# Fused bias, slope and maximum in two attention layers of a six-layer transformer kernel

## What is computed

```
# layer 3: 8 heads, two maps m per head, head width 64, values of width 128
p = masked_softmax(q_m @ k_m.T - slopes * dist, dist >= 0)
a = p[:, :, 0] - lam_full * p[:, :, 1]
o = rms_norm_2(a @ v, sub_gain) * (1.0 - lambda_init)      # per head of 128
return (o * silu(z)) @ w_out

# layer 4: 3 groups (w, d) = (128,1), (512,4), (2048,16), 4 heads, values of width 256
for each group:  s = q_g @ k_g.T - slopes * dist   on keys with dist <= w, dist % d == 0
                 e = exp(s - m);  l = sum(e);  out_g = (e / l) @ v;  lse_g = m + log(l)
o = sum_g softmax(lse)_g * out_g
return (o * silu(z)) @ w_out
```

## Time and profile before

| | us |
|---|---|
| median of 3 runs | 2045.27 (2043.88 to 2045.29) |
| the profiled execution | 2042.26 |
| its span | 2040.5 |
| TensorE busy | 1742.2 (85%), 9822 matmuls |
| VectorE busy | 1156.1 (57%), 1857 instructions |
| ScalarE busy | 970.5 (48%), 1683 instructions |
| GpSimd busy | 101.1 (5%) |

### The profile page before, as it was taken

One profiled execution on the slowest core, in us unless ns is written; L12 is line 12 of the kernel. 1 busy time (PEld: TensorE's weight loads), 2 busy tenths in 40 slices (PEclk: granted clock), 3 DMA queues, 4 the chain that ended last, 5 costly groups with the idle time before them and its releaser, 6 DMA issues.

```text
span 2040.5 us, 24999 instructions
## 1 busy us (share of the span) xinstructions
PE 1742.2 (85%) x9822; PEld 1379.4 (68%) x9822; DVE 1156.1 (57%) x1857; ACT 970.5 (48%) x1683; POOL 101.1 (5%) x135
## 2 busy tenths in 40 slices
PE   5996878994699973898899998988889969989987
PEld 2783447773577763666799997866678637757866
DVE  2217674446588865764566667435753484464454
ACT  5213223625588865464344443535555534544563
POOL 0000100001100002100000002000000000000000
PEclk7998888997899996999899998998999989999998
DMA  7224996011999982202255554432035303514521
GB/s 304 83 101 167 348 339 247 1 44 59 367 423 421 421 325 95 102 1 83 94 188 188 188 185 144 172 117 83 1 113 187 143 1 134 188 60 147 193 83 42
DMA packets 52691, 335.84 MB, mean 165 GB/s; under 512 B 5488, under 2 KB 5488, under 8 KB 18288
## 3 DMA queue, kind: packets, MB, share of 16 engines
q1 hardware_dynamic: 46112, 310.04, 40.6%
q0 software_dynamic: 6480, 24.44, 3.1%
HBM read 305.10 MB, written 29.36 MB: 164 GB/s over the span
## 4 chain that ended last, share of the span: by engine, by line
PE 66%; DVE 13%; ACT 10%; DMA 6%; issue 3%; POOL 1%; SPq 0%; POOLq 0%; DVEq 0%; ACTq 0%
PE bank L1235 17%; PE bank L1237 17%; PE bank L1236 17%; DMA ring_float<-weights_dram 4%; ACT hT_float L730 2%; DVE ring_float32r L2074 2%; ACT arena_float L784 2%; PE bank L1269 1%; PE bank L1432 1%; ACT ring_high L683 1%; PE bank L1558 1%; PE bank L1606 1%; PE bank L1550 1%; DVE stat L2741 1%; PE bank L1395 1%
## 5 line engine op out<-in xcount | busy, mean ns | idle before, releaser
L2074 DVE TENSOR_TENSOR ring_float32r<-ring_float,ring_high 128x1024 fp32r<-128x1024 f32 x298 | 355.3, 1230 | 369.3 <-ACT ring_high L683 369.1
L683 ACT ACTIVATE ring_high<-ring_float 128x1024 fp32r<-128x1024 f32 x298 | 301.4, 1059 | 412.9 <-DMA ring_float<-weights_dram 410.4
L1235 PE MATMUL bank<-ring_high,x_float32r 128*128 128x512 f32 x608 | 243.4, 400 | 5.6 <-DVE mix_float32r L2103 3.0
L1237 PE MATMUL bank<-ring_high,mix_float32r 128*128 128x512 f32 x608 | 241.2, 397 | 0.0
L1236 PE MATMUL bank<-ring_float32r,x_float32r 128*128 128x512 f32 x608 | 241.1, 397 | 0.0
L1235 PE MATMUL bank<-ring_high,arena_float32r 128*128 128x512 f32 (+1 forms) x368 | 139.6, 379 | 17.3 <-DVE arena_float32r L2103 6.6
L1235 PE MATMUL bank<-Z_float32r,ring_high 128*128 128x256 f32 x512 | 146.0, 285 | 8.0 <-issue 4.2
L1236 PE MATMUL bank<-Z_float32r,ring_high 128*128 128x256 f32 x512 | 146.1, 285 | 0.0
L1237 PE MATMUL bank<-Z_float32r,ring_float32r 128*128 128x256 f32 x512 | 145.9, 285 | 0.0
L1235 PEld LDWEIGHTS bank<-ring_high,x_float32r 128*128 128x128 f32 x608 | 116.0, 191 | 34.6 <-ACT hT_float L730 5.7
L1237 PE MATMUL bank<-ring_high,arena_float32r 128*128 128x512 f32 (+1 forms) x368 | 137.9, 375 | 0.0
(11 more groups left out here) (405 smaller groups left out, 3330.2 us busy)
## 6 DMA issues: line engine op xcount, KB each, us to landing
ring_float<-weights_dram SPq DMA_DIRECT2D x234, 1024.0 KB, 4.8
Z_float<-weights_dram SPq DMA_DIRECT2D x33, 1024.0 KB, 8.7
sent<-post_row SPq DMA_DIRECT2D x1, 11776.0 KB, 38.1
Z_float<-sent SPq DMA_DIRECT2D x23, 512.0 KB, 9.1
made<-mix_float POOLq DMA_DIRECT2D x23, 512.0 KB, 7.9
post_row<-norm_post_dram POOLq DMA_DIRECT2D x4, 512.0 KB, 4.4
small<-small_dram SPq DMA_DIRECT2D x1, 1072.0 KB, 9.2
x_float<-x_dram SPq DMA_DIRECT2D x1, 1024.0 KB, 5.3
```

Of the source, the lines that this page charges most:

```text
L683: nc.scalar.activation(ring_high[:, slot, half], ring[:, slot, half], ACT.Copy).then_inc(high_ready, 1)
L1235: nc.tensor.matmul(out, left[0], right[0], start=start, stop=False)
L1237: return nc.tensor.matmul(out, left[1], right[0], start=False, stop=stop)
L2074: ve.tensor_tensor(ring_low[:, slot, half], ring[:, slot, half], ring_high[:, slot, half], ALU.subtract).then_inc(low_ready, 1)
```

## The change

In layers 3 and 4, bias, slope and row maximum become one VectorE instruction, `tensor_tensor_reduce`: `out = (scores + bias) * (-slope)`, and the minimum of `out`, started from a given value, is written to one element per row. For this the queries are scaled by 1/slope when the banks are emptied (for each head, from a constant in layer 3 and from six new columns of the dilated table in layer 4), and the exponentials are taken with scale -1. A new pair of semaphores `e_full`, `e_free` (`E`, on the same banks 4 and 5) replaces `s_full`, `s_free` there; ScalarE waits for two releases instead of `max_ready`. In layer 4 the minimum of the first map starts the second's, and so on, each with a wait for the one before.

In layer 3 the squares and their sums by head move from VectorE to ScalarE (`head_sums`, four activations of 128 columns with accumulator, after steps 9, 13, 17 and at the end). VectorE's `squares` becomes `values`: reciprocal and scaling, a wait, and a one-element memset that tells ScalarE. The gain and `1 - lambda_init` are multiplied into silu(z) once, in the projection, after the low part of chunk 8 (two instructions of 1024 columns). The norm becomes four instructions of 128 columns, (value * root) * gated z, and comes one unit later.

In layer 4 VectorE no longer adds the three maps. TensorE multiplies the three maps by the identity into the same bank, summing them as it turns them (`turn_sum`), and waits for ScalarE's maps directly.

```diff
-DILATED, N_DILATED = fields([("dilated", 3 * LT * S), ("earlier_keys", P), ("later_sum", P), ("whole_sum", P)])
+DILATED, N_DILATED = fields([("dilated", 3 * LT * S), ("earlier_keys", P), ("later_sum", P), ("whole_sum", P),
+                              ("dilated_q", 6)])
...
+        E = Banks(bank[4:6], e_full, e_free)
...
+            def q_features_by(dst, n_ft, scale_of):
+
+                for j in range(n_ft // 2):
+                    drain(*[(dst[:, f * LT * P:(f + 1) * LT * P], lambda b, f=f: b[:, f % 2 * LT * P:(f % 2 + 1) * LT * P], scale_of(f), None)
+                            for f in (2 * j, 2 * j + 1)])
...
-                            q_features(aq, n_ft, LT, QSCALE)
+                            if i == 3:
+                                q_features_by(aq, n_ft, lambda f: QSCALE / alibi(8)[f])
+                            elif i == 4:
+                                act.wait_ge(dilated_loaded, 16)
+                                q_features_by(aq, n_ft, lambda f: dilated_q[:, f:f + 1])
...
+                def head_sums(g):
+
+                    act.wait_ge(head_values, g + 1)
+                    for n in range(4):
+                        at = slice(g % 2 * 512 + n * 2 * HD, g % 2 * 512 + (n + 1) * 2 * HD)
+                        m = nc.scalar.activation(weighed[:, n * 2 * HD:(n + 1) * 2 * HD], mix[:, g // 2, at], ACT.Square,
+                                                 accum_out=head_ss[:, 4 * g + n:4 * g + n + 1])
+                    m.then_inc(sums_ready, 1)
...
-                        seen.next(max_ready)
+                        seen.next(e_free, 2)
...
+                    if u >= 9 and u % 4 == 1:
+                        head_sums((u - 9) // 4)
+                head_sums(3)
...
+                def turn_sum(u, b):
+                    nk = P * (u // 4 + 1)
+                    for j in range(u // 4 + 1):
+                        for g in range(3):
+                            i = nc.tensor.matmul(b[:, j * P:(j + 1) * P], p_ring[u % 3][:, g * nk + j * P:g * nk + (j + 1) * P], ident,
+                                                 start=(g == 0), stop=(g == 2))
+                    return i
+
+                seen.next(maps_ready, LT * 8)
+                attend(LT * 4, score, turn_sum, weigh, maps_ready)
...
-                chunks_low(STREAM[f"in{i}"][0] + 1, 2 * IN_BLOCKS[i] - 1)
+                for c in range(1, 2 * IN_BLOCKS[i]):
+                    chunk_low(STREAM[f"in{i}"][0] + c)
+                    if i == 3 and c == IN_BLOCKS[i]:
+                        seen.next(z_act_ready)
+                        for t in range(LT):
+                            z = zs[3][:, t, GATE_AT[3]:GATE_AT[3] + D].rearrange("p (h d) -> p h d", d=2 * HD)
+                            m = ve.scalar_tensor_tensor(z, z, 1.0 - LAMBDA_INIT, under(sm("sub_gain"), 8), ALU.mult, ALU.mult)
+                        then(m)
...
-                        b = SC.filled_bank(dve)
-                        n = signal(ve.scalar_tensor_tensor(dst[:, m, :], bias, slope, b[:, 0:nk], ALU.mult, ALU.add), s_free)
-                    dve.wait_ge(s_free, n)
+                        b, n = E.filled_bank(dve), maps * u + m
+                        signal(ve.tensor_tensor_reduce(dst[:, m, :], b[:, 0:nk], bias, -slope, HUGE, ALU.add, ALU.min, nmax[:, n:n + 1]), e_free)
+                    return
...
-                    then(ve.tensor_tensor(weighed, group(g), group(g), ALU.mult))
-                    signal(ve.tensor_reduce(head_ss[:, 4 * g:4 * g + 4], weighed.rearrange("p (h d) -> p h d", h=4), AX.X, ALU.add),
-                           sums_ready)
...
+                    dve.wait_ge(v_free, own["v_free"])
+                    signal(ve.memset(lam[:, 7:8], 0.0), head_values)
...
-                    scale_heads(group(g), 4, 2 * HD, 4 * g)
-                    v = group(g).rearrange("p (h d) -> p h d", h=4)
-                    then(ve.scalar_tensor_tensor(v, v, 1.0 - LAMBDA_INIT, under(sm("sub_gain"), 4), ALU.mult, ALU.mult))
...
-                    gate(3, g // 2, g % 2 * 512, 512, g // 2 == LT - 1)
+                    for n in range(4):
+                        at = slice(n * 2 * HD, (n + 1) * 2 * HD)
+                        z = zs[3][:, g // 2, GATE_AT[3] + g % 2 * 512:GATE_AT[3] + g % 2 * 512 + 512]
+                        m = ve.scalar_tensor_tensor(group(g)[:, at], group(g)[:, at], head_rstd[:, 4 * g + n:4 * g + n + 1], z[:, at],
+                                                    ALU.mult, ALU.mult)
+                    signal(m, mix_ready if g // 2 == LT - 1 else dve_step)
...
-                    if u >= 7 and (u - 7) % 4 == 3:
-                        normed((u - 7) // 4)
+                    if u >= 8 and (u - 8) % 4 == 3:
+                        normed((u - 8) // 4)
...
+                    least = HUGE
...
+                            found = nmax[:, u:u + 1] if g == 2 else lam[:, g:g + 1]
+                            i = ve.tensor_tensor_reduce(s[:, g * nk:(g + 1) * nk], b[:, n * nk:(n + 1) * nk], dilated[:, g, qt, 0:nk],
+                                                        -slopes[g * 4 + h], least, ALU.add, ALU.min, found)
+                            if g < 2:
+                                then(i, dve_step if g == 0 else e_free)
+                            else:
+                                signal(i, e_free)
+                            least = found
-
-                def combine(u):
-                    nk = P * (u // 4 + 1)
-                    seen.next(maps_ready)
-                    p = p_ring[u % 3]
-                    then(ve.tensor_tensor(p[:, 0:nk], p[:, 0:nk], p[:, nk:2 * nk], ALU.add))
-                    signal(ve.tensor_tensor(p[:, 0:nk], p[:, 0:nk], p[:, 2 * nk:3 * nk], ALU.add), probs_mixed)
```

More of the change, by code:

```diff
@@ L38 @@
 TINY = 1e-30
+HUGE = 3e38
 HD = 64
@@ L170, in const_arrays @@
     dilated = np.concatenate([pack(dil), np.where(p[:, None] < p[None, :], 0.0, NEG), np.where(p[:, None] >= p[None, :], -1.0, 0.0),
[L171 removed]
+                              np.full((P, P), -1.0), QSCALE / np.array(alibi(12)).reshape(6, 2)[:, p // HD].T], 1)
     return [np.ascontiguousarray(a, np.float32) for a in (const, late, dilated)]
@@ L406, in build_program @@
         earlier_keys, later_sum, whole_sum = (rows[:, DILATED[n][0]:DILATED[n][1]] for n in ("earlier_keys", "later_sum", "whole_sum"))
+        dilated_q = rows[:, DILATED["dilated_q"][0]:DILATED["dilated_q"][1]]
         gate_rows = rows[:, :].rearrange("p (s n) -> p s n", s=2)
@@ L1175, in dilated_heads @@
                     if u < n_u:
-                        seen.next(max_ready)
+                        seen.next(e_free, 2)
                         nk = P * (u // 4 + 1)
-                        exp_probs(u, s_ring[u % 3][:, 0:3 * nk], p_ring[u % 3][:, 0:3 * nk], u).then_inc(maps_ready, 1)
+                        exp_probs(u, s_ring[u % 3][:, 0:3 * nk], p_ring[u % 3][:, 0:3 * nk], u, scale=-1.0).then_inc(maps_ready, 1)
                         out_high(4, u, n_u)
@@ L1922, in score @@
                     for m in range(2):
-                        b = SC.take(pe)
+                        b = E.take(pe)
                         nc.tensor.matmul(b[:, 0:nk], q8[rows_of(m), h, qt * P:(qt + 1) * P],
-                                         k8[rows_of(m), h, 0:nk], start=True, stop=True).then_inc(s_full, 1)
+                                         k8[rows_of(m), h, 0:nk], start=True, stop=True).then_inc(e_full, 1)
                 def weigh(u):
@@ L2883, in group, with values @@
                     return mix[:, g // 2, g % 2 * 512:g % 2 * 512 + 512]
-                def squares(g):
+                def values(g):
                     b = vbank()
                     then(ve.reciprocal(rsum[:, 8:12], sums[:, 8 * g:8 * g + 8:2]))
-                    then(ve.tensor_tensor(group(g).rearrange("p (h d) -> p h d", h=4), b[:, :].rearrange("p (h d) -> p h d", h=4),
-                                          over(rsum[:, 8:12], 2 * HD), ALU.mult), v_free)
-                    then(ve.tensor_tensor(weighed, group(g), group(g), ALU.mult))
-                    signal(ve.tensor_reduce(head_ss[:, 4 * g:4 * g + 4], weighed.rearrange("p (h d) -> p h d", h=4), AX.X, ALU.add),
-                           sums_ready)
+                    signal(ve.tensor_tensor(group(g).rearrange("p (h d) -> p h d", h=4), b[:, :].rearrange("p (h d) -> p h d", h=4),
+                                            over(rsum[:, 8:12], 2 * HD), ALU.mult), v_free)
+                    dve.wait_ge(v_free, own["v_free"])
+                    signal(ve.memset(lam[:, 7:8], 0.0), head_values)
                 def normed(g):
                     inv_root()
-                    scale_heads(group(g), 4, 2 * HD, 4 * g)
-                    v = group(g).rearrange("p (h d) -> p h d", h=4)
-                    then(ve.scalar_tensor_tensor(v, v, 1.0 - LAMBDA_INIT, under(sm("sub_gain"), 4), ALU.mult, ALU.mult))
-                    if g == 0:
-                        seen.next(z_act_ready)
```

(9 more changed lines are left out.)

20 lines of the change are left out of this document (8 added, 12 removed).

## The result

| | before | after |
|---|---|---|
| median, first comparison | 2043.56 us (6 runs, 2038.61 to 2045.29) | 2029.34 us (6 runs, 2023.92 to 2032.56) |
| span of the profiled execution | 2040.5 | 2028.1 |
| TensorE busy | 1742.2 | 1744.0 |
| VectorE busy | 1156.1 | 1132.4 |
| ScalarE busy | 970.5 | 977.2 |

The ratio is 0.993 (95% interval 0.9912 to 0.9948): faster by 0.7%, 14.2 us, where 6.6 were forecast and the range ended at 2034.0. Two later comparisons gave 0.9945 (0.9925 to 0.9964) and 0.9939 (0.9922 to 0.9957).

The account below looks back on a forecast made before the run. VectorE was taken to bound attention in layers 3 and 4, TensorE close behind in layer 4. -6.9 (layer 3), -0.5 (layer 4) and +0.8 (query drains) made -6.6 us: forecast 2038.7 against the 2045.27 median, range 2034 to 2044.5.

Parts of the forecast that it names:

- Scores of layer 3: Layer 3 scores on VectorE: fused instructions at 0.38 and 0.51 us replace biases and reduction, -0.7 and -3.0 us.
- Rival A: Fused instruction as cheap as the bias (0.28 and 0.41 us): 3.2 us more gain, -9.8, 2035.5 us; chance 0.14.
- Values and norms: Layer 3 group work on VectorE before the tail: values -2.3 us, norms as four 128-column instructions -1.7 us.
- The gain factor: Two 128x1024 instructions in layer 3's projection, some 1.25 us each, costing nothing because VectorE sits idle 2.98 us there.
- Cover: Layer 3 steps with ScalarE's new squares: ScalarE needs 3.2 us where VectorE gives 2.1; the second such step shows, +1.2 us.
- Tail: Uncovered chain after layer 3's last unit: VectorE's part falls 4.0 us, ScalarE's squares and hand-over return 3.6, so -0.4.
- Sum of layer 3: Layer 3 attention in all: -7.7 us before the tail, +1.2 for ScalarE's squares, -0.4 after the last unit, making -6.9.
- Layer 4: Layer 4 attention: 33.6 us to the last gate instead of 34.15, -0.5 us, with TensorE setting the pace in VectorE's place.
- rival D: Layer 4 gives the gain back: TensorE at half clock for 4 us costs 2 us more, -4.6 us; chance 0.08.
- Query drains: ScalarE empties each query bank in two pieces, 0.62 us instead of 0.50; seven banks in layers 3 and 4, +0.8 us.
- The yardstick: The unchanged kernel's median of three runs, 2045.27 us, against which the forecast time was set.

## Why the prediction was wrong

The direction of the whole, the two stages and, in layer 3, the mechanism were right; the size was not. By its own steps:

- **Scores of layer 3: the step that failed.** I took 0.38 and 0.51 us for a fused instruction, 0.10 over the bias, by ScalarE's accumulator read. From start to start it is 0.21 and 0.35. Two things were mis-sized. The result's row costs nothing, since the next instruction starts with it. And bias instructions without a wait between them already follow each other before they end, which I had used for the norm but not here: the pair of the earlier trace rows is 0.48 long, not 2 x 0.28. The term is 8 x 0.42 + 8 x 0.70 = -9.0 us where I had -3.7. Rival A, at 0.28 and 0.41, was nearest and still priced a pair at 0.56 and 0.82. With -9.0 in its place the forecast is 2033.4, below the range's lower end of 2034: that end was made with the length of one instruction for the distance between two. By the Trainium skill ("VectorE: DVE Perf Modes", section "Two Vector instructions with no wait between them") the fused one is two instructions; the trace has the two rows, and the measured distance of 0.35 us leaves nothing of the 0.57 that I worked out from it.
- **Values and norms:** -2.7 and -2.0 against -2.3 and -1.7; right within 0.7 together. The gain factor cost nothing in the projection, as said: VectorE's wait for ScalarE ahead of the next chunk shrank from 2.98 to 0.85 us and was not used up.
- **Cover:** +1.2, seen as exactly that wait. In the first units VectorE also came to wait for scores, 1.48 us in all; before the change it waited 1.34 there, 1.0 of it because of the half clock, so the sum below shows only 0.1 of this. No term was there for it.
- **Tail:** -2.0 against -0.4. VectorE's part fell by 2.3 a group (2.0 said), and the wait for ScalarE and GpSimd grew from 1.41 to 2.72, by 1.3 and not 1.8: the squares take 0.29 us each, not 0.39.
- **Sum of layer 3:** -9.0 - 2.7 - 2.0 - 2.0 + 1.2 + 0.1 = -14.4, where the windows have -14.2. About 1.0 of it is the half clock in the profile of the kernel before, not the change.
- **Layer 4:** at the full clock 33.3 us from first scores to last gate, where 33.6 was said. The turns are 0.67 and 1.34 us (0.68 and 1.36 said). So the rows that led to -0.5 were sound, and rival D named what the first profile then showed, with its place wrong: not where VectorE had held TensorE up before, but at the start, and for 4.6 us, not 2. What I had missed is that the two halves of this edit do not belong together: fusing alone makes it 32.65.
- **Query drains:** +0.8 said (a piece is 0.61, not 0.62, which makes it +0.7), next to nothing seen. ScalarE's drains took 4.25 us instead of 4.00, and TensorE's own transposes 3.42 instead of 3.18 beside them, so that its wait ahead of the last block of layer 3's projection is 0.36 us before and after. From the first transposes of queries and keys (1601.92 before, 1601.22 after) to the last block it is 5.81 us before and 5.88 after.
- **The yardstick:** the three runs shown had a median of 2045.27; six had 2043.56. That is 1.7 us of the 9.4 by which the forecast missed.

The missed 7.3 us of layer 3 are 5.3 from the fused instruction and 1.6 from the tail, the rest from values, norms and cover; the waits that came and the half clock that fell away in the first units nearly cancel. Open are whether waits start the half clock in layer 4, and whether VectorE's addition is the better kernel as a whole: its ratios were 0.9954 (0.9935 to 0.9972) and 0.9922 (0.9907 to 0.9936) in two comparisons, which straddle those of the changed kernel.

## To carry to other kernels

Price a short VectorE instruction by the distance from start to start in a run of its like, not by its length; with 256 and 128 columns the two differ by a sixth and a quarter, and a lower bound made of lengths is no bound. Before comparing two profiles of a stage, look where the half clock fell in each. When an edit has two halves, price each alone, and ask of the half that moves work to an engine already close to the bound what it costs at that engine's lower clock. When whole times scatter by several us, time the stage from its first instruction to the first one behind it.

## What had not been expected of the hardware

- A VectorE instruction that also reduces (two inputs, result and row minimum) costs 0.29 us at 128 columns and 0.42 at 256, and 0.21 and 0.35 from start to start. The bare bias is 0.28 and 0.41 long and 0.20 and 0.34 apart (pairs of 0.48 and 0.75 in the earlier trace rows), so the reduction costs 0.01 us. In layer 4, where each waits for the one before, the distance is 0.40 and 0.53:

```profile
1806.29 0.48 DVE L2976 CUSTOM_DVE_ANT_0 arena_float<-bank,rows,stat 128x256 f32<-128x256 f32 x1
1806.70 0.08 DVE L2976 DVE_READ_ACCUMULATOR2_ANT stat<- 128x1 f32 x1
1806.82 0.48 DVE L2976 CUSTOM_DVE_ANT_0 arena_float<-bank,rows,stat 128x256 f32<-128x256 f32 x1
```

- The same program with the same busy TensorE ran a stretch of ten microseconds at the half clock in one execution and at the full clock in another: 4.6 us of 2029.
